# Two transformer blocks: TensorE's code behind the experts' branch, compressed keys in split precision, and VectorE's order in the second attention

## What is computed

```python
x = x + 0.5 * swiglu(rms_norm(x, ffn1_norm), ffn1_w_in, ffn1_w_out)
proj = rms_norm(x, mix_norm) @ w_mix_in
o_a = banded_attention(q_a, k_a, v_a, tbl, WINDOW_A, sinks_a)       # kind 0, 8 heads
# compressed keys and values: 15 windows of 32 tokens, step 16, 64 columns each
pre = b1 + sum_over_window((kv + pos) @ w1)      # 2048 -> 128, for keys and for values, 2 groups
kv_c = silu(pre) @ w2 + b2
k_c, v_c = rms_norm(kv_c[0], k_norm_b), kv_c[1]
o_cmp, o_sel = nsa_cmp_sel(q_b, k_c, v_c, k_s, v_s, tbl_b)           # o_sel: kind 1
o_win = banded_attention(q_b, k_w, v_w, tbl_b, WINDOW_B, None)       # kind 2
o_b = gates[0] * o_cmp + gates[1] * o_sel + gates[2] * o_win
x = x + concat(o_a, o_b) @ w_mix_out
x = x + 0.5 * swiglu(rms_norm(x, ffn2_norm), ffn2_w_in, ffn2_w_out)
```

## Time and profile before

| | us |
|---|---|
| three runs | 1059.07, 1060.5, 1060.95 |
| median | 1060.5 |
| the profiled execution, device time | 1060.7 |
| its span in the trace | 1058.7 |
| PE busy | 1012.6 |
| VectorE busy | 734.1 |
| ScalarE busy | 609.1 |
| HBM, mean over the span | 210 GB/s |

### The profile page before, as it was taken

How to read it: one execution, slowest core, us unless ns; L and a number is a source line. 1 busy time by engine, 2 the same in 40 slices (tenths; PEclk the granted TensorE clock), 3 DMA queues, 4 the chain that set the end, 5 groups by cost and what they waited for, 6 DMA issues and landing times.

```text
span 1058.7 us, 13638 instructions
## 1 busy us (share of the span) xinstructions
PE 1012.6 (96%) x5237; PEld 844.4 (80%) x5237; DVE 734.1 (69%) x813; ACT 609.1 (58%) x694; POOL 51.7 (5%) x47
## 2 busy tenths in 40 slices
PE   7999999997899999999799999999998898999998
PEld 6788788787788888877578888897877687888887
DVE  5534885678999999999955556566487755555664
ACT  6476433538899999988743443345375345344331
POOL 0011561011000000000000000000000000000000
PEclk9999999997999999999999999999899999999999
DMA  8923444452999999999946555873420044555511
GB/s 297 336 83 120 134 145 150 148 186 85 320 373 386 387 386 386 386 386 387 346 145 202 195 191 167 281 271 126 157 80 2 1 159 164 197 194 193 174 70 40
DMA packets 117021, 223.29 MB, mean 211 GB/s; under 512 B 6426, under 2 KB 12713, under 8 KB 116970
## 3 DMA queue, kind: packets, MB, share of 16 engines
q1 hardware_dynamic: 116426, 221.08, 60.2%
q0 software_dynamic: 384, 1.24, 0.3%
q10 hardware_dynamic: 160, 0.27, 0.1%
HBM read 221.49 MB, written 1.07 MB: 210 GB/s over the span
## 4 chain that ended last, share of the span: by engine, by line
PE 79%; DVE 8%; DMA 7%; ACT 4%; issue 2%; DVEq 0%; ACTq 0%; SPq 0%
PE ps L1830 18%; PE ps L1832 18%; PE ps L1831 18%; DMA w_raw<-in_w_exp_gate 6%; PE ps L2127 5%; PE ps L2128 5%; DVE w_lo L965 3%; ACT w_hi L537 2%; PE ps L2151 2%; PE ps L2168 1%; PE ps L2381 1%; PE ps L1996 1%; DMA w_raw<-in_w_exp_down 1%; PE ps L1876 1%; PE ps L1825 1%
## 5 line engine op out<-in xcount | busy, mean ns | idle before, releaser
L965 DVE TENSOR_TENSOR w_lo<-w_raw,w_hi 128x2048 fp32r<-128x2048 f32 x204 | 464.7, 2289 | 144.3 <-ACT w_hi L537 140.6
L537 ACT ACTIVATE w_hi<-w_raw 128x2048 fp32r<-128x2048 f32 x204 | 390.9, 1917 | 215.8 <-PE ps L1832 199.5
L1830 PE MATMUL ps<-w_hi,h_hi 128*128 128x512 f32 (+1 forms) x704 | 273.6, 389 | 9.7 <-DVE h_lo L992 6.7
L1831 PE MATMUL ps<-w_lo,h_hi 128*128 128x512 f32 (+1 forms) x704 | 268.8, 382 | 0.0
L1832 PE MATMUL ps<-w_hi,h_lo 128*128 128x512 f32 (+1 forms) x704 | 268.7, 382 | 0.0
L1830 PEld LDWEIGHTS ps<-w_hi,h_hi 128*128 128x128 f32 x704 | 133.3, 189 | 38.0 <-issue 11.7
L1832 PEld LDWEIGHTS ps<-w_hi,h_lo 128*128 128x128 f32 x704 | 133.2, 189 | 26.0
L1831 PEld LDWEIGHTS ps<-w_lo,h_hi 128*128 128x128 f32 x704 | 133.4, 189 | 23.8
L1830 PE MATMUL ps<-w_hi,aT_hi 128*128 128x512 f32 x176 | 68.9, 391 | 0.0
L1832 PE MATMUL ps<-w_hi,aT_lo 128*128 128x512 f32 x176 | 68.5, 389 | 0.0
L1831 PE MATMUL ps<-w_lo,aT_hi 128*128 128x512 f32 x176 | 68.5, 389 | 0.0
(11 more groups left out here) (354 smaller groups left out, 1276.3 us busy)
## 6 DMA issues: line engine op xcount, KB each, us to landing
w_raw<-in_ffn_w_in SPq DMA_DIRECT2D x44, 1024.0 KB, 5.1
w_raw<-in_w_exp_gate SPq DMA_DIRECT2D x32, 1024.0 KB, 10.7
w_raw<-in_w_exp_up SPq DMA_DIRECT2D x32, 1024.0 KB, 9.8
w_raw<-in_w_exp_down SPq DMA_DIRECT2D x32, 1024.0 KB, 10.8
w_raw<-in_w_in SPq DMA_DIRECT2D x22, 1024.0 KB, 7.8
w_raw<-in_ffn_w_out SPq DMA_DIRECT2D x22, 1024.0 KB, 5.0
w_raw<-in_w_mix_in SPq DMA_DIRECT2D x8, 1024.0 KB, 6.3
w_raw<-in_w_out SPq DMA_DIRECT2D x4, 1024.0 KB, 5.0
```

The lines of the kernel that those rows point to most:

```text
L537: act.activation(w_hi[:, u % SPLIT, :], w_raw[:, u % RAW, :], ACT.Copy).then_inc(hi_ready, 1)
L965: dve.tensor_tensor(w_lo[:, u % SPLIT, :], w_raw[:, u % RAW, :], w_hi[:, u % SPLIT, :], ALU.subtract).then_inc(lo_ready, 1)
L1830: pe.matmul(out, hi, w_h, start=first, stop=False)
L1831: pe.matmul(out, hi, w_l, start=False, stop=False)
```

## The change

It has three parts.

1. On PE, all that follows the experts (first feed-forward to second feed-forward) becomes a function `behind_experts`. It is called at the end of the If body; in the Else body it is called too. The other engines' branches stay as they are.
2. The first weights of the compressed keys become two weight units, `U_CMP`, which pass through the ring and are split into high and low parts. The keys and values are split as well: ScalarE writes the high parts into `kv_cmp`, VectorE the low parts. PE now makes the data the stationary operand (128 columns: high and low, keys and values, 15 windows of each of two groups and the positions) and the weights the moving one (256 columns: key and value weights), in 2 x 16 matmuls (`compress`), half of them in front of mix unit (2,1) and half behind it. VectorE copies the sums out, and PE adds high and low rows with two matmuls against `fold` inside mix unit (3,0). Half of the products so computed (keys with value weights and the other way) are not used. The numbers of the units behind move up by two, and ScalarE and VectorE split the units in a new order around this.
3. In the attention loop VectorE does the merge ahead of `neg_logits` of its step, and `probs_T` ahead of most side work from step 8 on. The steps of the compressed attention move one later on PE (18 to 19, 20 and 22 to 21 and 23) and on VectorE (19, 21 and 23 to 20, 22 and 24), and the second half of the first outputs' low parts moves from step 16 to 17.

```diff
-U_MIXOUT = U_MIX + 8
+U_MIXOUT = U_MIX + 10
+U_CMP = (U_MIX + 5, U_MIX + 7)
...
+        kv_cmp = region_r("kv_cmp", 4096, PAIRS, 2, 2, 32)
+
+        def u_mix(i, kh):
+            return U_MIX + (0, 1, 2, 3, 4, 6, 8, 9)[2 * i + kh]
+
...
+        def kv_src(g, odd):
+
+            v = ps[g * DH:(g + 1) * DH, 4, :].rearrange("p (k s) -> p k s", k=2)
+            return bass.AP(v.tensor, v.offset + odd, [list(v.ap[0]), list(v.ap[1]), [CMP_STRIDE, N_CMP], [2, PAIRS]])
+
+        def kv_of(low, g, odd):
+
+            v = kv_cmp[odd * DH:(odd + 1) * DH, :, low, :, N_CMP * g:N_CMP * (g + 1)]
+            return v.rearrange("p pp k c -> p k c pp")
...
-            sp.dma_start(cmp_w1, a["cmp_w1_2"][0].rearrange("k (pp q) h -> q k pp h", q=P)).then_inc(cmp_in, 16)
             sp.dma_start(cmp_w2, a["cmp_w2_2"][0].rearrange("k q d -> q k d")).then_inc(cmp_in, 16)
...
+            def cmp_load(half):
+                u = U_CMP[half]
+                sp.wait_ge(lo_ready, u - RAW + 1)
+                dst = w_raw[:, u % RAW, :].rearrange("p (pp k h) -> p pp k h", k=2, h=P)
+                for kv, landed in enumerate((raw_in[u % RAW], cmp_in)):
+                    sp.dma_start(dst[:, :, kv], a["cmp_w1_2"][0, kv].rearrange("(pp q) h -> q pp h", q=P)[:, 8 * half:8 * half + 8]
+                                 ).then_inc(landed, 16)
+
+            for i in range(2):
+                for kh in range(2):
+                    mix_load(i, kh)
+            mix_load(2, 0)
+            cmp_load(0)
+            mix_load(2, 1)
+            cmp_load(1)
+            mix_load(3, 0)
+            mix_load(3, 1)
...
             split_hi(U_MIX + 4)
-            split_hi(U_MIX + 5)
+            act.wait_ge(cmp_in, 48)
+            split_hi(U_CMP[0])
+            act.wait_ge(kv_T, 1)
+            for g in range(2):
+                for odd in range(2):
+                    act.activation(kv_of(0, g, odd), kv_src(g, odd), ACT.Copy).then_inc(kv_hi, 1)
             leave_mix(1)
             split_hi(U_MIX + 6)
             head_rms(0, 16, 2)
-            split_hi(U_MIX + 7)
             act.wait_ge(gates_T, 2)
             for tt in range(TT):
                 ins = act.activation(gate_sig[:, tt, :], ps[:, 5, S + 32 * tt:S + 32 * tt + GATE_COLS], ACT.Sigmoid, scale=post[:, tt:tt + 1])
             ins.then_inc(gsig_ready, 1)
+            split_hi(U_CMP[1])
+            split_hi(U_MIX + 8)
+            leave_mix(2)
+            split_hi(U_MIX + 9)
             act.wait_ge(bias2_set, 1)
             for kv in range(2):
-                i = act.activation(hidT[:, kv, 0:30], ps[:, 4, 64 * kv:64 * kv + 30], ACT.Silu, bias=bias2[:, kv:kv + 1])
+                i = act.activation(hidT[:, kv, 0:30], ps[:, 4, S + 64 * kv:S + 64 * kv + 30], ACT.Silu, bias=bias2[:, kv:kv + 1])
             i.then_inc(hid_ready, 1)
-            leave_mix(2)
-            split_hi(U_MIX + 8)
+            split_hi(U_MIXOUT)
             head_rms(16, 24, 3)
-            split_hi(U_MIX + 9)
+            split_hi(U_MIXOUT + 1)
...
-            dve.wait_ge(pos_set, 2)
-            pos = kvT[:, :, 2, 0:2 * PAIRS].rearrange("p k (q two) -> p k q two", two=2)[:, :, :, 0]
-            dve.tensor_copy(pos, cols[:, ROW_POS:ROW_POS + 2 * PAIRS].rearrange("p (k q) -> p k q", k=2)).then_inc(kvT_ready, 1)
-            split_lo(U_MIX + 5)
+            dve.wait_ge(pos_set, 1)
+            pos = cols[:, ROW_POS:ROW_POS + 2 * PAIRS].rearrange("p (k q) -> p k q", k=2)
+            pos_hi, pos_lo = (kv_cmp[:, :, low, :, 2 * N_CMP:].rearrange("p pp k c -> p k pp c") for low in range(2))
+            for n in range(2):
+                dve.tensor_copy(pos_hi[:, :, :, n], pos).then_inc(kvT_ready, 1)
+            dve.wait_ge(kvT_ready, 2)
+            for n in range(2):
+                dve.tensor_tensor(pos_lo[:, :, :, n], pos, pos_hi[:, :, :, n], ALU.subtract).then_inc(kvT_ready, 1)
+            split_lo(U_CMP[0])
             dve.wait_ge(kv_T, 1)
-            kvp = ps[:, 4, :].rearrange("p (k s) -> p k s", k=2)
             for g in range(2):
-                src = kvp[g * DH:(g + 1) * DH]
-                dve.tensor_copy(kvT[0:DH, :, g, :], src).then_inc(kvT_ready, 1)
-                dve.tensor_copy(kvT[DH:P, :, g, 0:S - 1], src[:, :, 1:S]).then_inc(kvT_ready, 1)
+                dve.wait_ge(kv_hi, 2 * g + 2)
+                for odd in range(2):
+                    dve.tensor_tensor(kv_of(1, g, odd), kv_src(g, odd), kv_of(0, g, odd), ALU.subtract).then_inc(kvT_ready, 1)
             dve.wait_ge(gates_T, 1)
             dve.tensor_copy(gate_T, ps[0:GATE_COLS, 5, 0:S]).then_inc(gateT_set, 1)
             sum_blocks(1)
@@ -1593,18 +1632,22 @@
                 dve.tensor_scalar(q_gain[:, 2 * n:2 * n + 2], half_rows, cols[:, row:row + 1], DH ** -0.5, ALU.mult, ALU.mult).then_inc(q_gain_set, 1)
             inv_rms(0, 16, 1)
             scale_heads(0, 8, 8).then_inc(q_normed, 1)
-            split_lo(U_MIX + 7)
+            split_lo(U_CMP[1])
             dve.wait_ge(small_in, 64)
             chain(dve.tensor_scalar(nsink, sink, -1.0, None, ALU.mult))
+            split_lo(U_MIX + 8)
+            dve.wait_ge(unit_used, U_CMP[1] + 1)
+            dve.tensor_copy(cmp_sums.rearrange("p k h -> p (k h)"), ps[:, 4, 0:2 * P]).then_inc(kvT_ready, 1)
+            sum_blocks(2)
             dve.wait_ge(pre_T, 1)
-            pos_cols = ps[:, 4, 0:P].rearrange("p (k c) -> p k c", k=2)[:, :, 30]
+            pos_cols = ps[:, 4, S:S + P].rearrange("p (k c) -> p k c", k=2)[:, :, 2 * N_CMP]
             dve.tensor_tensor(bias2, pos_cols, cols[:, ROW_B1:ROW_B1 + 2], ALU.add).then_inc(bias2_set, 1)
-            split_lo(U_MIX + 8)
-            sum_blocks(2)
+            split_lo(U_MIX + 9)
             inv_rms(16, 24, 2)
             scale_keys(0, OFF_KA, 16)
             scale_heads(OFF_QB, 20, 4)
             scale_heads(OFF_QB + 256, 0, 4).then_inc(q_normed, 1)
+            split_lo(U_MIXOUT)
             dve.wait_ge(kvc_ready, 1)
...
-            split_lo(U_MIX + 9)
+            split_lo(U_MIXOUT + 1)
...
             for s in range(ITEMS + 4):
+                if s >= HEADS + 3 and (s - 3) % HEADS == 0:
+                    keep_kind((s - 3) // HEADS - 1)
                 if s < ITEMS:
                     neg_logits(s)
-                if s == 1:
-                    cmp_consts()
-                if s >= HEADS + 3 and (s - 3) % HEADS == 0:
-                    keep_kind((s - 3) // HEADS - 1)
-                if s == 16:
-                    cmp_gaps()
-                if s == 19:
-                    cmp_probs()
-                if s == 21:
-                    cmp_out(0)
-                if s == 23:
-                    cmp_out(1)
-                if s == HEADS:
-                    sink_diff()
                 if s == 0:
                     inv_rms(24, 30, 3)
                     scale_keys(1, OFF_KS, 24)
                 if s == 1:
+                    cmp_consts()
                     norm_cmp()
                 if s == 2:
                     scale_keys(2, OFF_KW, 28)
@@ -1784,12 +1816,22 @@
                 if s == 3:
                     kcT_out()
                     cmp_values()
+                if 2 <= s < ITEMS + 2:
+                    probs_T(s - 2)
+                if s == 16:
+                    cmp_gaps()
+                if s == 20:
+                    cmp_probs()
+                if s == 22:
+                    cmp_out(0)
+                if s == 24:
+                    cmp_out(1)
+                if s == HEADS:
+                    sink_diff()
                 if s == OA_STEP0 + 1:
                     transposed_lo(5, banks=OA_BANKS, steps=(0,))
-                if s == OA_STEP1 + 1:
+                if s == OA_STEP1 + 2:
                     transposed_lo(5, banks=OA_BANKS, steps=(1,))
-                if 2 <= s < ITEMS + 2:
-                    probs_T(s - 2)
...
+            def behind_experts():
+
+                def narrow(u, banks):
...
+                sums = ffn(U_FFN1, N_EXP, adds + 8, 13)
...
+                def compress(half):
+
+                    pe.wait_ge(lo_ready, U_CMP[half] + 1)
+                    for n in range(PAIRS // 2):
+                        pp, wc = 8 * half + n, slice(2 * P * n, 2 * P * (n + 1))
+                        rows = kv_cmp[:, pp].rearrange("p l k c -> p (l k c)")
+                        pe.matmul(ps[:, 4, 0:2 * P], rows, w_hi[:, U_CMP[half] % SPLIT, wc], start=(pp == 0), stop=False)
+                        i = pe.matmul(ps[:, 4, 0:2 * P], rows, w_lo[:, U_CMP[half] % SPLIT, wc], start=False, stop=(pp == PAIRS - 1))
+                    i.then_inc(unit_used, 1)
+
+                def fold_sums():
+
+                    pe.wait_ge(kvT_ready, 9)
+                    for kv in range(2):
+                        i = pe.matmul(ps[:, 4, S + 64 * kv:S + 64 * kv + 32], cmp_sums[:, kv, :], fold[:, 32 * kv:32 * kv + 32], start=True, stop=True)
+                    i.then_inc(pre_T, 1)
+
+                pe.wait_ge(kvT_ready, 8)
+                compress(0)
```

(19 more changed lines are left out.)

419 lines of the change are left out of this document (198 added, 221 removed).

## The result

The changed kernel takes 1048.53 us, the median of 4 runs (1047.78 to 1051.67); the kernel before takes 1060.72, the median of 4 (1059.07 to 1067.36). The ratio is 0.9871, 95% interval 0.9828 to 0.9914. The forecast was 1048.5. The sum came out right, its terms less so: the end of the program costs 1.7 to 2.0 us where 0.3 was forecast, the other two parts bring a little more, and the rest is what varies between executions.

The account below looks back on a forecast made before the run. PE, busy for 96% of the span, was taken as the bound, plus places where it stands still or runs slowly. Gains of 6.0 + 3.8 + 2.4 = 12.2 took 1060.7 to 1048.5 us, range 1045.8 to 1055.0.

Parts of the forecast that it names:

- Part 1, behind the experts: At the experts' end, PE's jump over the Else body goes: 4.6 us for the gap, 1.7 for the clock.
- The unexplained 4.7 us of the gap: Before the first feed-forward matmul, some 4.7 us of PE's gap had no operand behind it; taken as the jump.
- Part 1, the end: The jump moves to PE's last instruction at the program's end and costs 0.3 us there, bounds 0 and 1.9.
- Rival (c): At the program's end, the jump is as long as the first and costs 1.9 us: 1050.1, chance 0.09.
- the sign that the last rows would be PE's jump: At the program's end, last rows being PE's jump would show the prediction wrong.
- Part 2: Compressed keys by shorter matmuls: first minimum of the attention about 3.8 us earlier, bounds 2.0 and 5.5.
- the 8.6 forecast: Mix unit (2,1) on PE ends at 758.8 instead of 767.4, 8.6 us earlier.
- the queues: ScalarE's and VectorE's work behind mix unit (2,1), which shrinks PE's gain of 8.6 us to 3.8.
- The copies of 64x480: Compressed keys: four copies on ScalarE and four subtractions on VectorE, 2.4 to 5 us per engine, 2.4 taken.
- the 1 us that the prediction names as a sign of being wrong: Compressed keys: ScalarE's new copies taking over 1 us would show the prediction wrong.
- Part 3: VectorE's new order in the attention loop shortens PE's waits: 2.4 us, bounds 0.8 and 3.5.
- rival (d): Feed-forward loops inside the branch: six stalled backward jumps cost 41 us, giving 1089.5; chance 0.03.

Follow-up runs that it names:

- e5_before_short: The kernel before, with PE's all-experts body cut to one wait and the turning of the sums: 1054.95 us, ratio 0.995.
- e6_after_short: The changed kernel with PE's all-experts body cut the same way and without the second copy of the code behind the experts: 1046.68 us, ratio 0.9857.

## Why the prediction was right

**Part 1, behind the experts: right in both terms.** Forecast 4.6 for the gap and 1.7 for the clock; measured 4.53 and 1.69 to 1.70. The first matmul waits 0.67 for its low parts, as worked out from VectorE's four splits. The unexplained 4.7 us of the gap is the jump, which ends 0.14 before PE's next weight load. The mechanism is sharper than the text had it: not a jump, but one over a long body. The rule that the prediction took from the Trainium skill, "Runtime: NRT & Kernel Launch", section "Instruction fetch mechanics" (a taken branch outside the resident window waits for a fetch), fits `e5_before_short` and `e6_after_short`: with a short body the wait is nothing that can be seen. The prediction says that no row shows the fetch; the view of DMA does, as the packet above.

**Part 1, the end: the term was mis-sized, for want of a mechanism.** Forecast 0.3, bounds 0 and 1.9; measured 1.7 to 2.0 (5.24, 4.95, 5.06 and 5.04 against 3.25). The step that failed is that the end can only grow by PE's late arrival. That PE begins the jump early and is done in time was right, and more so than written: it begins 3.9 us ahead of the last add and takes 3.3 to 3.8, and PE is not late at all. That it is cheaper with DMA idle fits too: the instruction packet starts 0.95 to 1.0 us behind a jump at the entry or at the end, where DMA is nearly idle (shares 0.08 and 0.06 over that 1 us), and 3.5 to 3.6 behind one at the experts' end (share 0.94); place and share were not varied apart. What the text put at nothing is what a fetch does to others: it reads DMA as almost idle at the end, but the output's own transfer fills it there (share 1.05 over 1044 to 1046, first profile of the changed kernel), and the second fetch falls into it. Rival (c) has the right price, 1.9, by luck: its jump, as long as the first and ending behind everything else, did not happen. Nor did the sign that the last rows would be PE's jump; they are SyncE's wait for the output.

**Part 2: mechanism right, 0.7 too small.** Forecast 3.8, measured 4.48. The matmuls on PE cost what was forecast, 0.12 apart (timeline, first profile of the changed kernel):

```profile
744.62 0.28 PE L2376 MATMUL ps<-w_hi,kv_cmp 128*128 128x256 f32 x1
744.74 0.28 PE L2377 MATMUL ps<-w_lo,kv_cmp 128*128 128x256 f32 x1
```

The clock stays at 1.00 over 745 to 764, where it was 0.57 over 756 to 764. ScalarE's evacuation of mix group 2 starts 17.21 behind the key transposes (735.27 to 752.48, first profile of the changed kernel) against 25.13 (742.42 to 767.55): 7.9 of the 8.6 forecast. Behind it the queues took back 3.4 and not 4.8. The chain is the one walked: both table loads stand on it and VectorE waits for the roots (same profile).

```profile
756.73 1.28 ACT L932 ACT_TABLE_LOAD   x1
...
760.31 1.28 ACT L900 ACT_TABLE_LOAD   x1
...
761.94 0.25 DVE L1578 RECIPROCAL scalars<-scalars 128x16 f32<-128x16 f32 x1 [2.07 <-ACT scalars L900]
```

VectorE was forecast to go on with the roots at 768.7 on the old time base, which is 761.55 here (735.27 - 742.42 = -7.15 moves it), against 761.94 measured: 0.4 late. From there to the first minimum the text adds up 12.6 us of VectorE's steps; they took 11.5 (761.94 to 773.43), because it adds the durations as shown, and one step starts some 0.1 us before the one ahead of it is shown to end. That is the mis-sized term: 1.1 - 0.4 = 0.7. The copies of 64x480 took 1.02 each on ScalarE and 1.07 on VectorE, 4.1 and 4.3 in all, near the upper bound of 5 and not the 2.4 taken, and just over the 1 us that the prediction names as a sign of being wrong. PE's waits between 735 and 774 list none for them (0.2 for a low split is all that names another engine), so they cost little or nothing on the path.

**Part 3: right, 2.68 against 2.4.** The wait for probabilities goes, the merges' falls from 2.5 to 1.0, the one for compressed exponentials is no longer listed, and new waits of 0.6 (L1777), 0.4 more (L1789) and 0.4 more (low parts of the first outputs) appear. The text charged 0.5, 0.9 and 0.5 for them. What it lacked is the clock: profiles with this order show fewer falls in the attention, and the changed kernel can still lose 2.9 us at 778 to 786 (its first profile; 1.1 in two variants of it).

**The sum.** With measured terms at full clock 6.2 + 4.5 + 2.7 - 1.8 = 11.6, against 12.2. The profile's 1060.7 less 11.6 is 1049.1; the medians were 1048.53, 1048.95 and 1049.12. The end's 1.5 was made up by 0.7 and 0.3 elsewhere, and the last 0.6 is within what varies between executions (1047.8 to 1051.7). That the median met the forecast to 0.03 us is luck. Nothing was seen of rival (d): the stretch from the first feed-forward matmul to the keys is 212.7 with its loops inside the branch (changed kernel) and 212.72 with them behind it (`e5_before_short`), both at full clock behind the gap.

## What to carry to other kernels

A gap marked "issue" behind a branch that skips a long body can be the price of distance. Look for it where the likely path jumps, ask for the jump's own row and for packets of instructions in the view of DMA, and then let this path fall through, or shorten what it skips. The jump does not vanish when moved. Here it cost 6.2 us at the join (gap and clock), 3.65 more idle time at an entry with a wait of 2.0, and at the end nothing on PE but 1.7 to 2.0 through the output's transfer. So a distance that equals a known price is no proof of its cause: read what the last wait is. Where waits of 1 us go from PE's path the clock may give a second gain; here that is an inference from several profiles, and a single one can mislead by 3 us.

## What the runs showed of the hardware beyond what was expected

- A jump of PE over the all-experts body, alone or with all code behind the experts, takes 6.0 to 6.1 us at the join (three profiles), 3.68 at the entry (one) and 3.3 to 3.8 at the program's end (eight); over a body of one wait and the turning of the sums 0.17 to 0.18. Each long one contains one 16 KB packet of the instruction queue (0.9 to 1.4 us) and ends 1.4 us behind it.
- Such a packet amid the output's transfer puts off its landing: 4.5 to 4.9 us behind the last add in eight profiles, 2.84 to 2.86 in the six without it.
- The granted clock differs between executions of one program: the attention of the changed kernel took 53.65, 53.65 and 56.54 us, with PE busy for the same 9.57 of 12 us ahead of the place where one fell. Over the 25 runs of the kernel before beside the first group, the mean granted clock went from 0.974 (span 1069.1) to 0.989 (1055.6), some 0.9 us for each 0.001: most of this kernel's scatter goes with the clock.
- ScalarE and VectorE took 1.02 and 1.07 us for 64x480, written with 512-byte steps between single elements, where ScalarE takes 0.64 for a dense 128x512 (1.27 for two).
